# Second-layer weight sums of a two-level Winograd MLP moved from VectorE into adding DRAM transfers

## The reference, cut to what matters

```
h      = rmsnorm(x) @ w_in                      # projections, then attention and RWKV branches
x      = x + merged @ w_out
hm     = rmsnorm(x)                             # D = 1024
x      = x + square(relu(hm @ w_mlp_in)) @ w_mlp_out     # w_mlp_in 1024 x 4096, w_mlp_out 4096 x 1024
y      = rmsnorm(x)
```

## Time and profile before

| what | value |
|---|---|
| median of 3 runs | 2494.74 us (2493.43 to 2497.13) |
| the profiled execution's own time | 2478.53 us |
| its span, first to last instruction | 2476.8 us |
| TensorE busy | 2284.6 us, 92% |
| VectorE busy | 1603.3 us, 65% |
| ScalarE busy | 806.6 us, 33% |
| GpSimd busy | 434.4 us, 18% |
| mean granted TensorE clock | 0.969 of full |

### The profile page before, as it was taken

How to read it: one execution, slowest core, us unless ns; L and a number is a source line. 1 busy time by engine, 2 the same in 40 slices (tenths; PEclk the granted TensorE clock), 3 DMA queues, 4 the chain that set the end, 5 groups by cost and what they waited for, 6 DMA issues and landing times. The chain is left out here.

```text
span 2476.8 us, 48938 instructions
## 1 busy us (share of the span) xinstructions
PE 2284.6 (92%) x19275; PEld 1701.0 (69%) x19275; DVE 1603.3 (65%) x3005; ACT 806.6 (33%) x1425; POOL 434.4 (18%) x354
## 2 busy tenths in 40 slices
PE   6999999999899999898899889999999999989986
PEld 4566788765656566665665668787778778878865
DVE  3257888965556565345557556648975775776687
ACT  4235888424334342224455532111121111111101
POOL 0020000000000000001101102025354354344340
PEclk8989999999999999898999999999999999999998
DMA  6441232343232313247877744505226326315402
GB/s 188 121 119 63 64 104 71 122 151 102 57 102 59 97 47 105 76 109 225 284 244 258 235 177 148 170 21 200 81 65 191 102 65 184 109 56 178 124 1 81
DMA packets 270656, 306.78 MB, mean 124 GB/s; under 512 B 56230, under 2 KB 183047, under 8 KB 270300
## 3 DMA queue, kind: packets, MB, share of 16 engines
q1 hardware_dynamic: 195316, 252.78, 32.3%
q10 hardware_dynamic: 75112, 50.87, 7.3%
HBM read 239.78 MB, written 62.23 MB: 122 GB/s over the span
## 5 line engine op out<-in xcount | busy, mean ns | idle before, releaser
L1286 PE MATMUL rwkv_banks<-gate_sides_then_att_T 128*128 128x384 f32 (+1 forms) x768 | 280.4, 498 | 7.8 <-PEq L441 3.7
L1286 PEld LDWEIGHTS rwkv_banks<-gate_sides_then_att_T 128*128 128x128 f32 x768 | 139.4, 197 | 76.5 <-issue 19.4
L3606 DVE TENSOR_TENSOR merged_then_hidden<-merged_then_hidden,ps_mm 128x544 f32<-128x544 f32 x180 | 127.8, 715 | 81.9 <-PE ps_mm L3331 78.1
L3331 PE MATMUL ps_mm<-gate_sides_then_att_T,w_mm 128*128 128x272 f32 x584 | 147.6, 400 | 7.8 <-ACT merged_then_hidden L3399 5.4
L600 PE MATMUL first_banks<-hT,w_pr 128*128 128x384 f32 (+3 forms) x432 | 144.3, 491 | 4.6 <-PEq L188 4.6
L3331 PEld LDWEIGHTS ps_mm<-gate_sides_then_att_T,w_mm 128*128 128x128 f32 x584 | 113.0, 194 | 33.3 <-ACT merged_then_hidden L3399 5.8
L910 DVE TENSOR_SCALAR_CACHE_REDUCE _and_tildes_then_k_pages<-scores,mid 128x384 f32<-128x384 f32 (+4 forms) x150 | 131.5, 876 | 3.1
L600 PEld LDWEIGHTS first_banks<-hT,w_pr 128*128 128x128 f32 (+1 forms) x432 | 81.0, 192 | 62.2 <-issue 21.3
L3413 ACT ACTIVATE merged_then_hidden<-merged_then_hidden 128x1088 f32<-128x1088 f32 x32 | 35.6, 1111 | 260.6 <-DVE merged_then_hidden L3618 260.6
L3331 PE MATMUL ps_mm<-right_blocks,w_mm 128*128 128x272 f32 x408 | 101.8, 394 | 3.3 <-DVE sums_of_right_sides_ L3606 3.3
L2376 POOL MEMSET gate_sides_then_att_T<- 128x136 f32 x1 | 0.2, 212 | 596.3 <-POOLq L1181 596.3
(11 more groups left out here) (619 smaller groups left out, 5227.1 us busy)
## 6 DMA issues: line engine op xcount, KB each, us to landing
v_pages<-in_cache_v SPq DMA_DIRECT2D x128, 256.0 KB, 5.3
gate_sides_then_att_T<-in_w_in ACTq DMA_DIRECT2D x46, 512.0 KB, 4.3
_and_tildes_then_k_pages<-in_cache_k SPq DMA_DIRECT2D x88, 256.0 KB, 3.4
gate_sides_then_att_T<-right_blocks_d SPq DMA_DIRECT2D x82, 272.0 KB, 2.7
right_blocks<-right_blocks_d SPq DMA_DIRECT2D x65, 272.0 KB, 2.7
T_and_gates_then_weights<-in_w_mlp_in SPq DMA_DIRECT2D x16, 1024.0 KB, 5.2
T_and_gates_then_weights<-in_w_mlp_out SPq DMA_DIRECT2D x16, 1024.0 KB, 5.5
w_pr<-in_w_in SPq DMA_DIRECT2D x27, 512.0 KB, 5.2
```

What stands on the lines that cost most here:

```text
L1286: ins = MM(B[:, gate_bank(n), 0:w], gw[:, n % 2, k_, :], hc[:, k_, 0:w], start=(k_ == 0), stop=(k_ == KO - 1))
L3331: ins = nc.tensor.matmul(ps[:, bank, 0:272], w, right[:, k, :], start=(k == 0 and step in f.OPENS), stop=(k == 1), skip_group_check=True)
L3606: V.tensor_tensor(to, of, f.pair(ps, q, step), ALU.add).then_inc(f.by_dve, 1)
```

## The change

1. The outer left sums of the second layers (w_mlp_out) are no longer made on VectorE. A new DRAM tensor `sums_d` holds four 512 x 512 sums for each round. For each round, eight transfers issued by GpSimd make them: a copy and an adding transfer for each sum, in which s1 = a21 + a22, s3 = a21 + a11, s2 = s1 + a11, s4 = s2 + a12. Each waits on `w_sums` for the one before. Round 0's eight transfers are issued beside the projections, one for each pair of projection blocks. Those of rounds 1 to 3 are issued in rounds 0 to 2, one after each of `inner_sums(2)` to `inner_sums(9)` of the round.
2. SyncE loads seven pieces of 1 MiB for a second layer (a11, a12, a22 and the four sums) where it loaded four, each once its buffer's user in the layer before has finished. In second layers P6 and P3 exchange buffers (`left_2`).
3. `weight_sums` runs for the four first layers alone. As the new sums have other signs than the old, `spread_results` has the same count of additions and subtractions in other combinations.
4. `inner_sums(1)` moves from before the norm's last four additions to between the second and third of them.
5. The pieces of `hidden_sums` are due 2.8 us apart where they were 0.9 us, save t2 and t4 of the last round.

```diff
+    def add_in_dram(self, pool, w_2, r, n):
+        to = dict(zip(("s1", "s2", "s3", "s4"), self.sums_d[:, r]))
+        w = w_2.rearrange("(r k c) (m e) -> k m r c e", k=2, c=512, m=2)
+        a11, a12, a21, a22 = w[0, 0, r], w[1, 0, r], w[0, 1, r], w[1, 1, r]
+        name, *terms = (("s1", a21, a22), ("s3", a21, a11), ("s2", to["s1"], a11), ("s4", to["s2"], a12))[n // 2]
+        if self.sums_made:
+            pool.wait_ge(self.w_sums, 16 * self.sums_made)
+        if n % 2:
+            self.nc.gpsimd.dma_start(to[name], terms[1], accum_op=ALU.add).then_inc(self.w_sums, 16)
+        else:
+            self.nc.gpsimd.dma_start(to[name], terms[0]).then_inc(self.w_sums, 16)
+        self.sums_made += 1
...
+            for n in range(8):
+                pool.wait_ge(S["u_made"], 14 + 14 * n)
+                p.add_in_dram(pool, a["w_mlp_out"], 0, n)
+            pool.wait_ge(p.w_sums, 16 * p.sums_made)
...
-                    for name, user, sums in (("a11", "P1", 3), ("a12", "P2", 4), ("a21", "P7", 3), ("a22", "P4", 1)):
+                    for name in sorted(held if n % 2 else quarter, key=lambda name: order.index(user[name])):
                         if n:
-                            last = nth[n - 1][user]
+                            last = nth[n - 1][user[name]]
                             yield at(last, "P4") + STEP + 0.3
                             sp.wait_ge(*f.product(last, "P4"))
-                            sp.wait_ge(l_summed, 4 * (n - 1) + sums)
+                            if n % 2:
+                                sp.wait_ge(l_summed, 4 * r + {"a12": 4, "s2": 4}.get(name, 3))
...
-                        if n % 2:
+                        if n % 2 and name in summed_before:
+                            sp.wait_ge(p.w_sums, 128 * (r + 1))
+                            src = p.sums_d[summed_before.index(name), r]
...
             for n in range(4 * H2):
-                if n == 4 * H2 - 4:
-                    inner_sums(0)
-                    inner_sums(1)
+                if n in (4 * H2 - 4, 4 * H2 - 2):
+                    inner_sums((n + 4 - 4 * H2) // 2)
...
             for q in range(2, 14 * R):
                 inner_sums(q)
+                r, n = q // 14 + 1, q % 14 - 2
+                if r < R and 0 <= n < 8:
+                    p.add_in_dram(pool, w_2, r, n)
...
-                for n in range(2 * R):
+                for n in range(0, 2 * R, 2):
                     yield at(7 * n - 1, "P4") - 3.0 if n else -14.0
...
-                        yield at(at1 if n < 4 else at3, "P3") + STEP + 0.95 + 0.9 * (n % 4)
+                        yield at(at1 if n < 4 else at3, "P3") + STEP + 0.95 + (0.9 if r == R - 1 and n >= 4 else 2.8) * (n % 4)
...
-                            ch.done(V.tensor_tensor(to[:, rows, :], to[:, rows, :], of[:, rows, :], ALU.add))
+                            ch.done(V.tensor_tensor(to[:, rows, :], u[:, rows, :], v[:, rows, :], op))
```

More of the change, by code:

```diff
@@ L3073, in merge_and_mlp @@
     s4 = p.gate_side[:, 0:2048].rearrange("p (k c) -> p k c", k=H2)
+    held = {**quarter, "s1": s1, "s2": s2, "s4": s4}
+    summed_before = ("s1", "s4", "a21", "s2")
     left = {"P1": quarter["a11"], "P6": s2, "P7": quarter["a21"], "P4": quarter["a22"], "P5": s1, "P2": quarter["a12"], "P3": s4}
+    left_2 = {**left, "P6": s4, "P3": s2}
     inner = [t.rearrange("p (n k c) -> p n k c", n=4, k=2) for t in (d.w[:, 0, :], d.s[:, 0:2048])]
@@ L3100, in merge_and_mlp @@
     gate_in = [p.sem(f"mm_gate_in{n}") for n in range(2)]
-    q_in, q_scaled = ({n: p.sem(f"ml_{what}_{n}") for n in quarter} for what in ("in", "scaled"))
+    q_in = {n: p.sem("ml_in_" + n) for n in held}
+    q_scaled = {n: p.sem("ml_scaled_" + n) for n in quarter}
     moved = [p.sem(f"ml_moved{n}") for n in range(f.RING)]
@@ L3160, in weights @@
             def weights():
+                users = [{"a11": "P1", "a12": "P2", "a21": "P7", "s1": "P5", "a22": "P4", **more}
+                         for more in ({"s2": "P6", "s4": "P3"}, {"s4": "P6", "s2": "P3"})]
                 for n in range(2 * R):
-                    for name, user, sums in (("a11", "P1", 3), ("a12", "P2", 4), ("a21", "P7", 3), ("a22", "P4", 1)):
+                    r = n // 2
+                    order = layers[n - 1] if n else UP
+                    user = users[(n + 1) % 2]
+                    for name in sorted(held if n % 2 else quarter, key=lambda name: order.index(user[name])):
                         if n:
-                            last = nth[n - 1][user]
+                            last = nth[n - 1][user[name]]
                             yield at(last, "P4") + STEP + 0.3
                             sp.wait_ge(*f.product(last, "P4"))
-                            sp.wait_ge(l_summed, 4 * (n - 1) + sums)
+                            if n % 2:
+                                sp.wait_ge(l_summed, 4 * r + {"a12": 4, "s2": 4}.get(name, 3))
                         else:
@@ L3224, in inner_sums @@
             def inner_sums(q):
-                base, to = left[names[q]], inner[q % 2]
+                base, to = (left, left_2)[q // 7 % 2][names[q]], inner[q % 2]
                 def free(step):
@@ L3278, in product @@
             def product(q, step):
-                name, base, e = names[q], left[names[q]], inner[q % 2]
+                name, base, e = names[q], (left, left_2)[q // 7 % 2][names[q]], inner[q % 2]
                 r, first_layer = q // 14, q % 14 < 7
@@ L3646, in spread_results @@
                 last = nth[2 * R - 1]
[L3647 to L3650 removed]
+                for after, step, sums in (("P1", "P4", ((x11, x11, y1, ALU.add),)),
+                                          ("P5", "P4", ((x12, x12, y5, ALU.subtract), (x22, x22, y5, ALU.add))),
+                                          ("P6", "P4", ((y6, y6, y1, ALU.subtract), (x12, x12, y6, ALU.subtract))),
+                                          ("P7", "P4", ((y7, y6, y7, ALU.subtract),)),
+                                          ("P4", "P3", ((x21, x21, y7, ALU.add), (x22, x22, y7, ALU.add)))):
+                    for n, (to, u, v, op) in enumerate(sums):
                         for m, rows in enumerate((up, down)):
```

39 lines of the change are left out of this document (18 added, 21 removed).

## The result

The median after is 2449.03 us (four runs, 2444.02 to 2457.41), beside 2494.09 us (four runs, 2492.65 to 2497.13) for the kernel before: a ratio of 0.983, interval 0.9802 to 0.9859.

The account below looks back on a forecast made before the run. VectorE, overfull where second layers begin, was taken to hold TensorE, which otherwise sets the pace. Gains of 21.0 + 3.9 + 4.7 = 29.6 us took the median from 2494.7 to 2465 us, range 2455 to 2483.

Parts of the forecast that it names:

- These 42.5 us are all that the change can reach: MLP start, second-layer beginnings, t2 and t4: TensorE's idle and low-clock losses there, 42.5 us, were the most to gain.
- Outer left sums, 21.0 us: Second-layer beginnings: taking 16 additions off VectorE removes most of TensorE's waits, 21.0 us (bounds 12 and 24).
- 0.7 us a round: Second-layer beginnings: waiting still left in each round after the outer left sums move, 0.7 us (bounds 0 and 3).
- t1 and t3 move as well; t3's second half is then due 5.7 us later, and its product's first step 12 us after that, so nothing waits for it.: Hidden sums t1 and t3: spacing them delays nothing, and no gain was counted for it.
- if VectorE's order and not its load held the banks: Second-layer beginnings: a sign that the prediction is wrong, PSUM banks held by VectorE's order; no size given.
- t2 and t4, 3.9 us: Hidden sums in rounds 0 to 2: spacing t2 and t4 gains 3.9 us (bounds 1.5 and 5.7).
- The 0.6 us I left in each round: t2 and t4 in rounds 0 to 2: waiting that stays after spacing, 0.6 us a round.
- The start, 4.7 us: Start of the MLP: moving `inner_sums(1)` gains 4.7 of 8.8 us (bounds 3.5 and 8.8).
- Loads and transfers, 0: Second-layer loads and adding transfers: hidden behind other work, cost 0; DMA load cost 0 (bound 5 us).
- the 13.8 us of cover: Ring loads in SyncE's queue: issued early enough that 13.8 us cover a 5.5 us delay from a 1 MiB load.
- a cost from 15.6 on: Waits on `w_sums`, rounds 0 to 2: rival of GpSimd held by transfers, costing time from 15.6 us each; chance 0.09.
- the waits removed are in both, so the median goes from 2494.7 to 2465.1: Whole run: the 29.6 us taken off the profiled execution come off the median in full, 2494.7 to 2465.1 us.

Follow-up runs that it names:

- no_spacing: The kernel after with the hidden sums' old due times, 0.9 us apart everywhere: 2469.47 us, 0.9917 of the kernel before.
- space_t1_t3: The kernel after with t1 and t3 spaced 2.8 us, t2 and t4 at the old 0.9 in every round: 2458.93 us, 0.9889 of the kernel before.
- inner_only: The kernel before with only `inner_sums(1)` moved between the norm's last additions: 2485.87 us, 0.9973 of the kernel before.
- no_inner: The kernel after with `inner_sums(1)` in its old place: 2462.3 us, 0.9882 of the kernel before.
- after_again: The kernel after, unchanged, profiled once more: 2452.21 us, 0.9848 of the kernel before.
- no_transfers: The kernel after without its 32 copying and adding transfers, loading plain corners of w_mlp_out in place of the sums: 2452.02 us, 0.9858 of the kernel before.
- all_at_once: The kernel after with the eight transfers of a round issued in a row behind `inner_sums(2)`: 2581.29 us, 1.0386 of the kernel before.
- spacing_only: The kernel before with only the new due times of the hidden sums: 2488.44 us, 0.9984 of the kernel before.
- better_tail: The kernel after with round 3's t2 and t4 and the additions of `spread_results` spaced too: 2444.64 us, 0.984 of the kernel before.
- tail_again: better_tail unchanged, run on another chip: 2455.97 us, 0.9869 of the kernel before.
- better_both: better_tail with layer 0's third left sum due at 17.0 instead of 12.0: 2446.12 us, 0.9842 of the kernel before.
- better_start: better_both with t4 of the merge's own sums 5.3 us later: 2447.05 us, 0.9848 of the kernel before.

## Why the prediction was wrong

The main mechanism was right: second-layer beginnings were held by a full VectorE. Three things were wrong. Terms of the sum were too small; the part of the change that earns much of the gain was put at nothing; and the step from the sum to the median had no room for how whole runs differ. By the prediction's own steps:

**What bounds the kernel.** "These 42.5 us are all that the change can reach" looks like the 42.1 us of TensorE's waits, but that is chance. The 42.5 are 34.0 us of idle time and 8.5 of low clock in the stretches named. The waits are 42.1 over the whole part: four of them, 3.3, 0.8, 0.6 and 2.1 us at the end of the MLP, lie outside those stretches and are still there after the change.

**Outer left sums, 21.0 us.** The full VectorE was the cause, as the stretches at 32.00 of 32.00 show. This term took part 1 as a whole, with t1 and t3 already spread, and left 0.7 us a round. Measured, the move alone takes 13 to 14 us of waits and 16.8 us of the two-level part; the spacing of t1 and t3 takes 5.3 us of waits on top. The 0.7 us are not there in rounds 0 to 2. In round 3 two waits of 1.0 and 0.8 us are left, 2.2 us with the steps around them, for 2.8 forecast.

**A step that failed: "t1 and t3 move as well; t3's second half is then due 5.7 us later, and its product's first step 12 us after that, so nothing waits for it."** I asked who waits for t3, and not what waits behind it on VectorE. The results do, and TensorE behind them. I had read the same pattern at t2 and t4 and priced it at 2.1 us, and I had written that t1's halves would lengthen once GpSimd is free; put together, they give `no_spacing`'s waits of 2.12 us, three of them, two with slow steps behind. All spacing together was worth 9.7 us of waits and 18.4 us of the two-level part, most of the difference low clock, where the sum had 3.9. This moves gain from one part of the change to another. It does not by itself make the total wrong, as the 21.0 us had t1 and t3 spread. The prediction's last sign of being wrong, "if VectorE's order and not its load held the banks", came half true: the load held them before, and with the load gone the order would have.

**t2 and t4, 3.9 us.** The waits of 1.5, 2.1 and 2.1 us in `space_t1_t3` are all gone in the kernel after: 5.7, my upper bound. The 0.6 us I left in each round are not there, as the halves took 1.8 and 1.7 us and not 2.05. Both residues, 4 x 0.7 and 3 x 0.6, are 4.6 us that the sum withheld, and nearly all of it was gained. That is about the difference between 29.6 and the 33.8 of the first pair of profiles. That it fits within half a microsecond is luck, as the low clock alone differs by more between executions.

**The start, 4.7 us.** Measured over the first 20 steps it is 4.3 to 4.9 us between before and `inner_only`, and 3.2 to 3.8 between `no_inner` and the kernel after. ScalarE's first copy in the kernel after stands right behind the matmul; its timeline answers to the earlier trace rows:

```profile
1685.61 1.21 ACT L3412 ACTIVATE gate_sides_then_att_T<-x 128x544 f32<-128x544 f32 x2 [5.44 <-DVE x L2982]
1686.97 0.61 ACT L3431 COPY merged_then_hidden<-ps_mm 128x544 f32<-128x544 f32 x1 [0.15 <-PE ps_mm L3363]
```

The next thing late is VectorE, as said: it takes its first result 7.2 us after the part's first matmul (at 1692.14), for 11.1 before. TensorE's timeline there:

```profile
1697.87 2.00 PE L3363 MATMUL ps_mm<-x,T_and_gates_then_weights 128*128 128x272 f32 x8
1702.27 3.76 PE L3363 MATMUL ps_mm<-gate_sides_then_att_T,w_sums_mm 128*128 128x272 f32 x8 [2.41 <-DVE merged_then_hidden L3635]
1705.87 2.00 PE L3363 MATMUL ps_mm<-gate_sides_then_att_T,T_and_gates_then_weights 128*128 128x272 f32 x8
```

A wait of 2.41 us is left, and a step behind it that took 1.76 us longer. Where that step ran at full clock, as in `after_again`, a further wait of 0.73 us followed, so at this place the clock cost some 0.7 us and not 1.8.

**Loads and transfers, 0.** Right for the transfers by `no_transfers`; for the loads by the first layers, where TensorE is busy 50.00 of 50.00 us. The DMA issues of the kernel after in the two-level part (count, size, median us to landing) answer to the earlier trace rows:

```profile
sums_of_w_mlp_out_d<-in_w_mlp_out POOLq DMA_DIRECT2D x18, 1024.0 KB, 9.5
right_blocks<-right_blocks_d SPq DMA_DIRECT2D x65, 272.0 KB, 3.6
T_and_gates_then_weights<-in_w_mlp_out SPq DMA_DIRECT2D x12, 1024.0 KB, 8.9
```

The ring's loads land in 3.6 us for 2.7, well inside the 13.8 us of cover. GpSimd hardly waits for a transfer: once, 1.2 us, in the whole kernel. The 24 in the MLP took 9.2 us in the mean and at most 14.0, and the eight beside the projections at most 14.5, where the prediction had 11 and a cost from 15.6 on. In its timeline in round 1 both issues follow without idle time.

```profile
1966.44 0.54 POOL L86 DMA_DIRECT2D sums_of_w_mlp_out_d<-sums_of_w_mlp_out_d  x1
...
1979.27 1.02 POOL L84 DMA_DIRECT2D sums_of_w_mlp_out_d<-in_w_mlp_out  x1
```

The Trainium skill (SBUF — State Buffer, SBUF: two separate sides) says that GpSimd cannot write descriptors while VectorE runs an instruction in a 2-port mode and holds the shared port. No sign of it here, though no run shows whether these additions are of that kind: issues take 0.5 to 1.0 us beside a VectorE that is nine tenths busy, and the stage is no longer than without them. The lock rule of the Trainium skill (SBUF — State Buffer, Who interferes with whom) agrees in direction with t1's halves at 1.8 us for 1.25. It did not take 10 us back: with the spacing the results stand between the longer halves, and without it the waits of 2.1 us appear.

**From the sum to the median, the step that put the time outside the range: "the waits removed are in both, so the median goes from 2494.7 to 2465.1".** The two-level part gained 33.8 us in the first pair of profiles and 35.2 by the mean of all (779.9 to 744.7), 4 to 6 us over 29.6. Taken from 2494.7, 33.8 us would give 2461, inside the range. The medians of the three comparisons gained 45.1, 36.7 and 31.7 us. The range's lower end was made of the same bounds as the sum, and an interval of a ratio here is 0.3% to each side, 7 us; the range gave that nothing. So it is partly luck on which side of 2455 a median falls: the three of the kernel after are 2449.0 and 2452.2, below the range, and 2458.7, inside it. Whether the first 45 us hold something beyond the stage stays open: no profile shows it.

## What to carry to other kernels

When a piece of work is moved in an engine's order, ask not only who waits for its result but what stands behind it on that engine; on a nearly full engine that second question had the larger price. When one load is taken away, look at what the freed partner engine will now lengthen, and read whether the next place then has the pattern of a wait that the trace already shows and prices. To tell parts of some microseconds apart, take the waits in a stage first, which repeated within about 1 us here; then its length, which differed by 4.5 us between executions of one kernel, with the clock. Take whole runs for the claim that a kernel is faster.

## What was not expected of the hardware

- A transfer in DRAM that adds 1 MiB onto a sum took 9.4 to 14.0 us in the MLP of the kernel after, 11.2 in the mean. A copy out of the weights took 7.9 to 8.9 us (8.4), and a copy from one sum to another, contiguous in DRAM, 5.2 to 7.0 us (5.8). So adding costs some 3 us more than copying, and not three times as much. In `all_at_once` the intervals from issue to issue were 8.1, 13.8, 9.6, 11.7, 5.4, 9.1 and 5.5 us, copy and adding transfer in turn. Issuing takes GpSimd 0.5 to 0.9 us for a copy and 1.0 for an adding transfer.
- After a wait of TensorE the clock falls sometimes. The 2.41 us in the kernel after and the 4.13 us in `spacing_only` were followed by a step of 3.76 us, at 1.2 GHz; the 3.25 us in `better_tail` by one of 2.10, at 2.4 GHz. The same wait of 3.25 us stands in four profiles: the step behind it took 2.10 us in `better_tail` and `tail_again`, and 4.00 and 3.99 us in `better_both` and `better_start`. This is TensorE's timeline in `better_both`:

```profile
2349.29 4.00 PE L3363 MATMUL ps_mm<-right_blocks,w_sums_mm 128*128 128x272 f32 x8 [3.25 <-DVE x L3635]
```

So the same wait may cost some 2 us more or not, and removing waits gave up to 7.3 us in this way beside the 26.5.
